# Two ordinary pairs instead of three at the head of each feed-forward layer, with the token-half sums in another order

## What is computed

```
def swiglu_ffn(x, w_in, w_out):
    g, u = jnp.split(x @ w_in, 2, axis=-1)      # w_in is 1024 x 5632: gate part and up part
    return (jax.nn.silu(g) * u) @ w_out         # w_out is 2816 x 1024

xp = xp + swiglu_ffn(rmsnorm(xp, ffn_norms[i]), *ffn_params[i])
```

## Time and profile before

| what | value |
|---|---|
| median of 3 runs | 2556.8 us (2554.12 to 2557.77) |
| the profiled execution | 2556.29 us, span 2554.5 us |
| PE busy in the span | 2535.4 us, 99% |
| DVE busy | 1725.4 us, 68% |
| ACT busy | 1198.0 us, 47% |
| granted TensorE clock, mean | 0.998 |

### The profile page before, as it was taken

The page is one execution under the profiler, slowest core; times in us unless marked ns, Lnnn a source line. Parts: engine busy times, 40 slices in busy tenths (PEclk is TensorE's granted clock), DMA queues, the critical chain, the costliest instruction groups (busy, mean ns, idle before and its releaser), DMA issues.

```text
span 2554.5 us, 48137 instructions
## 1 busy us (share of the span) xinstructions
PE 2535.4 (99%) x19981; PEld 2470.7 (97%) x19981; DVE 1725.4 (68%) x2533; ACT 1198.0 (47%) x1806; POOL 171.0 (7%) x182
## 2 busy tenths in 40 slices
PE   8999999999999999999999999999999999999998
PEld 8999999999988899999998899999999999999998
DVE  5555794985555589589557556958955565884973
ACT  5544551543555455245346544524534553642543
POOL 2101000001000020000122210000011101000001
PEclk9999999999999999999999999999999999999999
DMA  3222333332433233323322232332323223333332
GB/s 114 76 69 83 108 89 101 99 87 80 121 101 100 81 92 100 108 83 95 88 74 73 73 91 83 100 108 83 95 81 88 71 69 91 104 89 92 106 89 79
DMA packets 441747, 230.68 MB, mean 90 GB/s; under 512 B 16996, under 2 KB 438081, under 8 KB 441553
## 3 DMA queue, kind: packets, MB, share of 16 engines
q1 hardware_dynamic: 439904, 226.90, 30.9%
q10 hardware_dynamic: 1200, 0.59, 0.1%
q0 software_dynamic: 448, 0.45, 0.1%
HBM read 219.03 MB, written 8.87 MB: 89 GB/s over the span
## 4 chain that ended last, share of the span: by engine, by line
PE 96%; DVE 2%; issue 1%; ACT 0%; DMA 0%; SPq 0%; DVEq 0%; ACTq 0%
PE slot L2300 53%; PE aux L2779 17%; PE slot L2779 15%; PE aux L2268 2%; PE aux L2300 2%; PE aux L2681 1%; PE aux L2445 1%; PE aux L2687 1%; PE aux L2593 1%; PE aux L2531 1%; PE aux L2460 1%; DVE w_lo L1417 0%; PE aux L2463 0%; PE slot L2308 0%; DMA x_rows<-in_x_prompt_dram 0%
## 5 line engine op out<-in xcount | busy, mean ns | idle before, releaser
L2300 PE MATMUL slot<-xg_hi,w_hi 128*128 128x272 f32 x1792 | 388.3, 298 | 3.9 <-DVE gla_sq L1435 2.2
L737 ACT ACTIVATE w_hi<-raw 128x1024 fp32r<-128x1024 f32 (+4 forms) x217 | 250.6, 1155 | 291.2 <-PE slot L2300 272.1
L2300 PE MATMUL slot<-xg_hi,w_lo 128*128 128x272 f32 x1792 | 371.1, 289 | 0.0
L2300 PE MATMUL slot<-xg_lo,w_hi 128*128 128x272 f32 x1792 | 370.9, 288 | 0.0
L1417 DVE TENSOR_TENSOR w_lo<-raw,w_hi 128x1024 fp32r<-128x1024 f32 (+4 forms) x215 | 291.9, 1358 | 67.3 <-ACT w_hi L737 66.8
L2300 PEld LDWEIGHTS slot<-xg_hi,w_hi 128*128 128x128 f32 x1792 | 281.5, 189 | 15.5 <-issue 9.2
L2300 PE MATMUL slot<-h_hi,w_hi 128*128 128x272 f32 x1386 | 286.1, 288 | 0.6 <-issue 0.6
L2300 PE MATMUL slot<-h_hi,w_lo 128*128 128x272 f32 x1386 | 285.8, 287 | 0.0
L2300 PE MATMUL slot<-h_lo,w_hi 128*128 128x272 f32 x1386 | 285.5, 287 | 0.0
L2300 PEld LDWEIGHTS slot<-xg_lo,w_hi 128*128 128x128 f32 x1792 | 282.1, 189 | 0.0
L2300 PEld LDWEIGHTS slot<-xg_hi,w_lo 128*128 128x128 f32 x1792 | 281.2, 189 | 0.0
(11 more groups left out here) (392 smaller groups left out, 5950.9 us busy)
## 6 DMA issues: line engine op xcount, KB each, us to landing
raw<-in_l_ffn_w_out_dram SPq DMA_DIRECT2D x64, 704.0 KB, 4.7
raw<-in_l_ffn_w_in_dram SPq DMA_DIRECT2D x60, 512.0 KB, 5.0
raw<-in_l_gla_w_in_dram SPq DMA_DIRECT2D x48, 512.0 KB, 3.9
ffn_raw_b<-in_l_ffn_w_in_dram SPq DMA_DIRECT2D x80, 256.0 KB, 3.4
ffn_raw_b<-in_l_ffn_w_in_dram SPq DMA_DIRECT2D x40, 512.0 KB, 5.2
raw<-in_l_ffn_w_in_dram SPq DMA_DIRECT2D x72, 256.0 KB, 3.2
raw<-in_l_att_w_qkv_dram SPq DMA_DIRECT2D x24, 512.0 KB, 3.8
raw<-in_l_lru_w_in_dram SPq DMA_DIRECT2D x24, 512.0 KB, 3.8
```

Of the source, the lines that this page charges most:

```text
L737: act.activation(w_hi[par][:, 0:kt, :], raw[par][:, 0:kt, :], ACT.Copy).then_inc(s_hi, 1)
L2300: ins = pe.matmul((slot[par] if bank is None else bank)[:, hf, 0:HALF], w[par][:, k, :], a[:, k0 + k, hf * HALF:(hf + 1) * HALF], start=(k ...
```

## The change

The string of the first half gets one S more (`UP_PAIRS[0]` from CCC... to CC...): pair 2 becomes a seven-product pair in each of the 4 layers. For this the token-half sums must be done a window earlier, and the four steps are put in another order: `t_x(2)`, `t_x(3)` and `t_sum(2)` go into window 0, `t_sum(3)` and all of `t_high` and `t_low` of q = 2 and 3 into window 1. The counting tables follow. PE's wait for s_rstd at pair 2 now stands before a seven-product pair.

```
-UP_PAIRS = ("CCCSSSSSSSS", "SSSSSSSSSSS")
+UP_PAIRS = ("CCSSSSSSSSS", "SSSSSSSSSSS")
-T_X_AT, T_HI_AT = (1, 2, 5, 6), (3, 4, 7, 8)
-T_SUM_AT, T_LO_AT = (0, 3, 8, 11), (7, 8, 15, 16)
+T_X_AT, T_HI_AT = (1, 2, 4, 6), (3, 5, 7, 8)
+T_SUM_AT, T_LO_AT = (0, 3, 7, 11), (7, 11, 15, 16)
@@ ACT, up_window
                 if now == "S" and nxt == "S":
                     hi_sums((i, hf, u + 1), b + 2, now)
+                if hf == 0 and u == 0:
+                    t_high(i, 0)
                 if hf == 0 and u == 1:
-                    t_x(i, 2)
-                    t_x(i, 3)
                     t_high(i, 2)
+                    t_high(i, 3)
...
                     split(b + 2, p0, XT if nxt else FH)
-                if hf == 0 and u < 2:
-                    t_high(i, (0, 3)[u])
                 if hf == 0 and u == 0:
+                    t_x(i, 2)
                     t_high(i, 1)
+                    t_x(i, 3)
@@ DVE, up_window
                 if hf == 0 and u == 1:
-                    t_sum(i, 2)
                     t_sum(i, 3)
                     t_low(i, 2)
+                    t_low(i, 3)
...
                 if hf == 0 and u == 0:
                     t_low(i, 0)
+                    t_sum(i, 2)
                     t_low(i, 1)
-                if hf == 0 and u == 1:
-                    t_low(i, 3)
@@ PE
                         elif kind == "S":
+                            if hf == 0 and u == 2:
+                                pe.wait_ge(s_rstd, stat_of[i, "ffn"] + 1)
                             seven_products(i, hf, u, b)
```

## The result

| what | before | after |
|---|---|---|
| median of 22 runs each, on one chip | 2556.34 us (2553.9 to 2558.49) | 2562.31 us (2558.56 to 2565.37) |
| profiled execution | 2556.29 us | 2563.16 us, span 2561.4 us |
| FFN stretch of a layer (below), layers 0 to 3 | 370.41, 370.41, 369.09, 368.94 | 371.33, 372.74, 370.03, 369.88 |

What follows compares the result with a forecast made beforehand. PE, 99% busy, was taken to bound the kernel. Per layer 2.27 us of wait less 1.49 saved gives +3.1 us in all, plus 3.0 for the clock: 2562.4 us from 2556.3, range 2557.8 to 2566.0.

Steps and rivals of the forecast that it cites:

- What the change removes: Pair 2 on PE: 12 matmuls fewer in each of 4 layers, 1.49 us each, 5.96 us in all.
- Window 0 is free: Window 0: the moved ACT and DVE steps are hidden, with 0.5 us to spare at the silu; cost nothing.
- Window 1 pays: Window 1: DVE's gapless 10.88 us chain makes PE wait 2.3 us at pair 2 in each layer.
- One of the prediction's own signs: Window 1, profile after: DVE's product of pair 0 should start 11.2 us ahead of the first low parts' end.
- No second wait, nothing given back: Behind pair 2's start: later operands are ready in time, so no second wait, and none of the 2.3 us returns.
- The clock: Behind the four waits at pair 2: PE's clock falls after two, 1.5 us each, +3.0 us.
- My reason for two of four: Ahead of the earlier kernel's two long waits PE has light work, at pair 2 dense matmuls; so two falls, +3.0 us.
- Three places: Trace before: three waits to judge the clock by; it fell after 2.17 and 1.90 us, not after 1.08.
- The waits come, the clock holds: Rival at pair 2: the waits appear without any clock fall, 2559.4 us; chance 0.20.
- Four falls: Rival at pair 2: clock falls after every wait, or each wait is 0.3 us longer as well; 2565.5 us; chance 0.12.
- Covered: Rival at pair 2: DVE finishes the first low parts by 288.3, no wait, a gain to 2550.3 us; chance 0.07.
- wait near the saving: Rival at pair 2: a wait of 1.2 to 1.9 us, clock held, 2555 to 2558 us; chance 0.06.

Runs made afterwards that it cites:

- The runs with a shorter and a longer wait: Changed kernel: DVE's scaling, or scaling and h's low part, behind the first low parts, 2555.62 and 2555.76 us; one more DVE addition before the weight sums, 2573.63 us.
- the last variants: Changed kernel, q = 3 low part behind the weights' first low parts, 2552.16 and 2551.88 us; then the third block's low part before pair 1's product, 2551.85 us.
- the first GpSimd run: Changed kernel with the scaling and low part of h moved later, and the third token-half sum's low part made by GpSimd: 2561.73 us.
- the run with the filled wait: Changed kernel with 17 more matmuls of 272 columns, results overwritten, just ahead of PE's wait at pair 2 of each layer: 2560.15 us.

## Why the prediction was right

It gave 2562.4 us, slower by 0.24%; measured were 2562.3 us, and 0.20% and 0.28% in two sets of runs. By its own steps:

**What the change removes.** 1.49 us a layer. PE has 48 matmuls less, and with the wait taken away pair 2 is shorter by 1.24 us, the missing 0.25 being the hold inside it; the layers are shorter by 1.23 to 1.34. (In layer 0, which gained 1.34, the eight pairs behind show 10.53 us each where they had 10.55; why is not shown.) The term was right for the changed kernel itself, which has no such hold.

**Window 0 is free.** Without the offset of 1.34 us the silu ended at 278.97 (predicted 279.0), the product of pair 0 started at 279.61 (279.55), and the low part behind it ended at 281.47 (281.4). `t_high(0)` waited 0.46 us (0.4). The run with the order alone shows that all of it costs nothing.

**Window 1 pays.** From the start of the product to the end of the first low parts 10.90 us (10.88). PE's wait shows 2.17 us in the brackets; pair 2 started 2.33 us later than before within the layer and lasted 0.07 us longer than its twins, so 2.40 in all where I had 2.27. The difference of 0.13 is made of the release, 0.14 us instead of 0.05, the end of the low parts, 0.08 later (0.06 of it at the product's start), and the restart, 0.07 or 0.08 instead of 0.11. The runs with a shorter and a longer wait moved the wait by what DVE's chain got or lost, to within 0.1 us. One of the prediction's own signs did not fit its sum: it asked for 11.2 us from the start of the product to the end of the low parts, where the sum had 10.88.

**No second wait, nothing given back.** The waits have no other line in windows 1 to 3, and the pairs behind pair 2 stay later by the same amount to the end of the layer. But the prediction looked only at the second low parts inside pair 2, not at those of the third and fourth blocks. Those are in time here because PE comes 2.3 us late; the last variants, where it does not, show the hold of 0.25 us.

**The clock.** This was the step that I had least ground for. The mechanism is as told: behind a wait of 2.17 us the clock falls in some layers and not in others, and not in the same ones each time, and one fall costs 1.37 to 1.41 us over the layer (predicted 1.5; 1.54 in the first GpSimd run, 372.70 beside 371.16). The number of falls was put too high: I said two of four; each of the two profiles has one, and the medians (6.0 - 3.7 = 2.3 us) come to 1.6 at most, since this takes all that is left for clock. In the first profile the stretches between the layers' blocks grew by 0.4 us as well, and no run isolates why. Over the four profiles with waits of 1.87 to 2.17 us it fell behind 6 of 16.

My reason for two of four was that PE has light work ahead of the two long waits of the kernel before. For the one at 29.67 that was a thin reading. Its last two rows ahead of the wait:

```profile
26.74 0.41 PE L2300 MATMUL slot<-xg_hi,w_lo 128*128 128x272 f32 x2
26.99 0.51 PE L2268 MATMUL aux<-ident,vec_rows 84*128 84x84 f32 x3
```

Only some 0.5 us of small transposes lie between matmuls of 272 columns and the wait. "Three places" was also incomplete: PE waited 1.87 us at 13.43 and 0.92 at 15.06 too, and the clock was at 0.50 from 15.94 to 19.35. So no run shows that the kind of work ahead of the wait decides. What they show is that one and the same wait can go either way, and that the number of falls was a guess that came near.

The two sizes erred in opposite directions, the wait by +0.6 us (3.7 instead of 3.1) and the clock by -0.7 us (2.3 instead of 3.0). That the total came out within 0.1 us is luck; that it came out slower by some 0.2% is not.

**The rivals.** "The waits come, the clock holds" is what the run with the filled wait is: 2.8 us above the kernel before, where the changed kernel is 6.0 and 6.2. The stretches at 946.20 and 1583.40 show that the clock does fall behind waits of 2.17 us. They disagree with the rule that the prediction cited from the Trainium skill, page "TensorE: Matmul & The Clock Gate", section "Why this matters for your kernels", which asks to avoid only gaps of more than about 3 us between bursts of matmuls. "Four falls" is what the run with 3.5 us waits showed, not this one. "Covered" and "wait near the saving" came about too, but only in the variants in which DVE's order is changed.

## What to carry to other kernels

When PE is 99% busy, less work on PE buys time only if the engine that prepares the operands can be ready earlier; add up that engine's instructions from the last thing it cannot start sooner, by start-to-start steps, and compare with PE's arrival. A wait costs its length plus, at 1.9 to 2.2 us in this kernel, a chance of a clock fall (6 of 16) worth 1.4 us more. If the chain is late, look which of its instructions the first matmuls do not need: here, moving three of them behind the one that PE was waiting for turned +6.0 us into -4.2 to -4.8.

## What the runs showed of the hardware that I had not expected

- GpSimd and VectorE held each other up for whole instructions: 0.44 us became 2.80 and 0.69 became 2.92 on VectorE, and 2.53 became 3.40 on GpSimd. Work given to an idle GpSimd took 2.2 to 2.4 us from VectorE, where VectorE itself needs 1.2 for it. The same thing stands in the trace of the kernel before, and I had read past it. There VectorE and GpSimd have, just ahead of layer 0's block (the last row of DVE is a later one of the same form, with GpSimd idle):

```profile
258.68 1.51 DVE L1429 SCALAR_TENSOR_TENSOR xg_lo<-x,vec_a,xg_hi 128x544 fp32r<-128x544 f32 x1 [1.37 <-ACT xg_hi L740]
...
264.66 0.79 DVE L1429 SCALAR_TENSOR_TENSOR xg_lo<-x,vec_a,xg_hi 128x544 fp32r<-128x544 f32 x1
```

```profile
258.24 1.37 POOL L2881 TENSOR_TENSOR sq_sum<-sq_sum,sq_x 128x544 f32<-128x544 f32 x1 [4.64 <-ACT sq_x L755]
```

DVE's instruction at 258.68 began while GpSimd's was at work until 259.61, and took 1.51 us, where the same form alone takes 0.79.

- At pair 2 the clock fell more often the longer the wait, within a narrow range: behind none of the eight waits of 0.9 and 1.5 us, 6 of 16 of 1.87 to 2.17, and all four of 3.5. These are few waits, and the length of a single one is not all: at the program's start the clock also fell behind two waits of 1.87 and 0.92 us close together, and behind the wait of 2.2 to 2.4 us there it fell in some profiles and not in others. Behind the waits of 3.5 us the low stretch was twice as long in two of the four (6.8 instead of 3.4 us) and cost 2.4 to 2.5 us instead of 1.4.
- PE does not speed up at once after a release: the first matmul behind a wait at full clock lasted 0.36 us instead of 0.29, and the next started 0.21 us after it instead of 0.13 (292.20 after 291.99).
